# A fused first norm, a new order before w_o, and a last norm without GpSimd, in a two-block transformer on one Trainium2 core

## The reference, cut to what matters

```python
# 1. the first norm, and the input of all projections
u = rmsnorm(x, norm_mix) * (1.0 + scale1) + shift1      # shift1, scale1: first two rows of silu(c) @ ada_w + ada_b
... = split_cols(u @ w_in)                              # u is 512 x 1024
# 2. gates and branches, and the projection behind them
y_b = dsa_attention(...) @ w_br_b                       # 256 -> 1024
merged = gates[0] * y_a + gates[1] * y_b + gates[2] * y_c   # gates = sigmoid(u @ w_in[:, gates] + gate_b)
x = x + gate1 * (merged @ w_o)
# 3. the last norm
h = layer_norm(ALPHA * h + sq_relu_mlp(h, w1, w2), ln_g, ln_b)   # the output, 512 x 1024
```

## Time and profile before

| | us |
|---|---|
| median of 3 runs | 2599.14 |
| the three runs | 2591.30, 2599.14, 4247.02 |
| the profiled execution | 2593.75 |
| its span, first to last instruction | 2592.0 |
| TensorE busy (98%) | 2534.8 |
| VectorE busy (58%) | 1492.3 |
| ScalarE busy (44%) | 1144.0 |
| GpSimd busy (18%) | 454.5 |

### The profile page before, as it was taken

The page is one execution under the profiler, slowest core; times in us unless marked ns, Lnnn a source line. Parts: engine busy times, 40 slices in busy tenths (PEclk is TensorE's granted clock), DMA queues, the critical chain, the costliest instruction groups (busy, mean ns, idle before and its releaser), DMA issues.

```text
span 2592.0 us, 34147 instructions
## 1 busy us (share of the span) xinstructions
PE 2534.8 (98%) x13495; PEld 2126.6 (82%) x13495; DVE 1492.3 (58%) x2850; ACT 1144.0 (44%) x2214; POOL 454.5 (18%) x526
## 2 busy tenths in 40 slices
PE   6999999999999999999999999999999999999998
PEld 5876777798888988887897988889788887988888
DVE  5376977565433499888774743334735744743333
ACT  3365544354332435554654543324543553643322
POOL 4133342200000146553000100000000100100001
PEclk8999999999999999999999999999999999999999
DMA  9432234434433333213431333333221442333332
GB/s 271 122 98 74 66 100 122 120 94 127 130 95 94 90 90 98 58 58 94 129 87 50 89 98 98 98 98 88 82 82 33 130 123 57 90 98 97 96 93 89
DMA packets 470432, 253.02 MB, mean 98 GB/s; under 512 B 16458, under 2 KB 464670, under 8 KB 470271
## 3 DMA queue, kind: packets, MB, share of 16 engines
q1 hardware_dynamic: 466975, 243.18, 32.9%
q0 software_dynamic: 3152, 7.59, 1.3%
q10 hardware_dynamic: 144, 0.07, 0.0%
HBM read 247.99 MB, written 2.80 MB: 97 GB/s over the span
## 4 chain that ended last, share of the span: by engine, by line
PE 86%; DVE 6%; issue 3%; ACT 3%; DMA 1%; POOL 1%; SPq 0%; DVEq 0%; POOLq 0%; ACTq 0%
PE ps L1030 21%; PE ps L1032 20%; PE ps L1038 20%; PE ps L951 3%; PE ps L949 3%; PE ps L947 3%; PE ps L1188 1%; PE ps L965 1%; PE ps L1531 1%; PE ps L1553 1%; PE ps L967 1%; PE ps L978 1%; PE ps L1203 1%; DMA w_f<-in_w_in 1%; DVE w_r L2587 1%
## 5 line engine op out<-in xcount | busy, mean ns | idle before, releaser
L1030 PE MATMUL ps<-XH,wh 128*128 128x512 f32 (+2 forms) x1896 | 758.5, 400 | 8.6 <-ACT wh L1748 5.1
L1032 PE MATMUL ps<-XL,wh 128*128 128x512 f32 x1776 | 697.0, 392 | 0.5 <-DVE XL L2904 0.5
L2587 DVE TENSOR_TENSOR w_r<-w_f,wh 128x512 fp32r<-128x512 f32 (+1 forms) x625 | 409.2, 697 | 467.7 <-ACT wh L1748 467.1
L1748 ACT ACTIVATE wh<-w_f 128x512 fp32r<-128x512 f32 x787 | 446.3, 616 | 358.7 <-PE ps L1038 195.9
L1038 PE MATMUL ps<-XH,w_r 128*128 128x512 f32 (+2 forms) x1896 | 494.6, 392 | 2.9 <-DVE w_r L2587 2.9
L1030 PEld LDWEIGHTS ps<-XH,wh 128*128 128x128 f32 (+2 forms) x1896 | 356.7, 188 | 102.6 <-issue 16.0
L1038 PEld LDWEIGHTS ps<-XH,w_r 128*128 128x128 f32 (+2 forms) x1896 | 355.6, 188 | 82.7 <-DVE w_r L2587 5.6
L1032 PEld LDWEIGHTS ps<-XL,wh 128*128 128x128 f32 x1776 | 334.1, 188 | 73.3 <-issue 1.9
L1032 PE MATMUL ps<-arena_r,wh 128*128 128x512 f32 (+1 forms) x936 | 326.1, 359 | 0.0
L3758 POOL TENSOR_TENSOR w_r<-w_f,wh 128x256 fp32r<-128x256 f32 (+1 forms) x314 | 236.5, 784 | 362.8 <-ACT wh L1748 362.7
L1030 PE MATMUL ps<-arena_r,wh 128*128 128x512 f32 (+1 forms) x726 | 253.1, 363 | 2.6 <-ACT wh L1748 2.6
(11 more groups left out here) (430 smaller groups left out, 3654.6 us busy)
## 6 DMA issues: line engine op xcount, KB each, us to landing
w_f<-in_mlp_w SPq DMA_DIRECT2D x126, 512.0 KB, 4.1
w_f<-in_w_ff SPq DMA_DIRECT2D x63, 512.0 KB, 4.1
w_f<-in_w_in SPq DMA_DIRECT2D x49, 512.0 KB, 3.8
w_f<-in_ada_w SPq DMA_DIRECT2D x35, 512.0 KB, 4.1
w_f<-in_even_w_in SPq DMA_DIRECT2D x35, 512.0 KB, 3.7
w_f<-in_odd_w_in SPq DMA_DIRECT2D x23, 512.0 KB, 3.8
w_f<-in_even_w_out SPq DMA_DIRECT2D x16, 512.0 KB, 4.1
w_f<-in_xa_w_v SPq DMA_DIRECT2D x16, 512.0 KB, 4.1
```

Of the source, the lines that this page charges most:

```text
L1030: e.matmul(b, hi[:, k, :], xh, start=u.first and k == 0, stop=False)
L1032: e.matmul(b, hi[:, k, :], xl, start=False, stop=False)
L1748: e.activation(high_flat(u)[:, s], flat(u, 0)[:, s], ACT.Copy).then_inc(act.sem, act.up("high", u.n, i))
L2587: e.tensor_tensor(low[:, s], raw_[:, s], high[:, s], ALU.subtract).then_inc(dve.sem, dve.up("low", u.n, i))
```

## The change

Opening: VectorE forms hT x gain x root in one instruction and GpSimd's pass is gone; the shift is added by ScalarE while it rounds and by VectorE while it subtracts. ScalarE rounds both first weight blocks ahead of the chunks; VectorE lowers the first before the modulation is finished. TensorE does its second `mod_rows` ahead of the strip products. The 18 late loads move from ahead of project unit 2 to ahead of unit 6, the packs' turning from behind part 2 to behind part 7. Before w_o: the order becomes out 8, gate 12, ada, out 9, out 10, gate 13, ada, out 11, ada, out 12, gate 14, out 13, gate 15, out 14, out 15, and the splitting of `merged` and of the first w_o blocks is interleaved by hand behind gate 15. End: all eight second passes are on VectorE, in a new order. Context lines are left out in most places.

```diff
@@ -81,7 +81,6 @@
-SHARED_OUT = ((1, 0), (1, 1), (3, 0))
@@ -301,10 +300,8 @@
-    plans["branch b"] = []
-    for j in range(4):
-        plans["branch b"] += [b_outs[j], b_gates[4 + j]] + ([next(rest)] if j < 3 else [])
-    plans["branch b"] += b_outs[4:]
+    o, g = b_outs, b_gates
+    plans["branch b"] = [o[0], g[4], next(rest), o[1], o[2], g[5], next(rest), o[3], next(rest), o[4], g[6], o[5], g[7], o[6], o[7]]
...
     def before_norm(stage, units):
@@ -628,8 +625,8 @@
-        merged_after = {("gate", 2 * KC - 1): (0, 1), ("branch", KC + 4): (2, 3), ("branch", KC + 5): (4,),
-                        ("branch", KC + 6): (5,), ("branch", KC + 7): (6, 7)}
+        last_gate, last_outs = plans["branch b"][-3], plans["branch b"][-2:]
+        first_outs = plans["w_o"][:2]
@@ -755,7 +752,6 @@
-        out_by = lambda t, half: pool if (t, half) in SHARED_OUT else dve
@@ -870,7 +866,7 @@
-                if u is plans["project"][2]:
+                if u is plans["project"][6]:
@@ -889,7 +885,7 @@
-                w.wait_ge(out_by(t, half), "out", t, half)
+                w.wait_ge(dve, "out", t, half)
@@ -1154,6 +1150,7 @@
+            mod_rows(rows_bank, 1)
@@ -1162,8 +1159,6 @@
-            mod_rows(rows_bank, 1)
@@ -1174,7 +1169,7 @@
-                if i == 2:
+                if i == 7:
@@ -1732,6 +1727,13 @@
             def copy(o, i, *mark, scale=1.0):
...
+            def round_piece(u, i):
+                w.wait_ge(d_raw[u.raw], "unit", u.n)
+                w.wait_ge(pe, "unit", u.high_before.n)
+                s = slice(i * HIGH_PIECE, (i + 1) * HIGH_PIECE)
+                e.activation(high_flat(u)[:, s], flat(u, 0)[:, s], ACT.Copy).then_inc(act.sem, act.up("high", u.n, i))
...
             def round_ahead(n):
@@ -1998,12 +2000,12 @@
-            round_ahead(plans["mod"][-4].n)
+            round_ahead(plans["mod"][-1].n)
...
-                e.activation(XH[:, k, :], normed[:, k, :], ACT.Copy).then_inc(act.sem, act.up("xh", "X0", k))
-                if k == 0:
-                    round_ahead(plans["mod"][-1].n)
+                w.wait_ge(dve, "mod", 15)
+                e.activation(XH[:, k, :], normed[:, k, :], ACT.Identity, bias=shift(0, k), scale=1.0).then_inc(
+                    act.sem, act.up("xh", "X0", k))
@@ -2115,10 +2117,21 @@
-            for u in plans["branch b"]:
-                run_steps([u])
-                for k in merged_after.get((u.name, u.m), ()):
-                    merged_high(k)
+            run_steps(plans["branch b"][:-3])
+            round_ahead(last_gate.n)
+            assert units[rounded[0]] is first_outs[0]
+            rounded[0] += 2
+            merged_high(0)
+            for u in first_outs:
+                round_piece(u, 0)
+            evacuate(last_gate)
+            merged_high(1)
+            merged_high(2)
+            round_piece(first_outs[0], 1)
+            merged_high(3)
+            round_piece(first_outs[1], 1)
+            for k in range(4, KC):
+                merged_high(k)
@@ -2545,12 +2558,6 @@
-            def token_scaled(t, half):
-                w.wait_ge(dve, "out centered", t, half)
-                w.wait_ge(act, "token rstd", t // 2)
-                e.activation(ot_part(t, half), ot_part(t, half), ACT.Copy, scale=token_rstd[:, t:t + 1]).then_inc(
-                    act.sem, act.up("out scaled", t, half))
@@ -2559,13 +2566,10 @@
-            token_scaled(1, 0)
...
-            token_scaled(1, 1)
...
-            token_scaled(3, 0)
...
         def vector_program(e):
@@ -2573,6 +2577,13 @@
+            def lower_piece(u, i):
+                w.wait_ge(act, "high", u.n, i)
+                s = slice(i * HIGH_PIECE, (i + 1) * HIGH_PIECE)
+                e.tensor_tensor(flat(u, 1)[:, s], flat(u, 0)[:, s], high_flat(u)[:, s].bitcast(F32), ALU.subtract).then_inc(
+                    dve.sem, dve.up("low", u.n, i))
...
             def lower_ahead(n):
@@ -2880,6 +2891,14 @@
+            def scaled(k):
+                w.wait_ge(act, "rstd", "mix")
+                w.wait_ge(pe, "q", "mix")
+                w.wait_ge(dve, "gain", 0)
+                e.scalar_tensor_tensor(out=normed[:, k, :], in0=hT[:, k, :], scalar=gain(0, k), in1=stat[:, 0, :],
+                                       op0=ALU.mult, op1=ALU.mult).then_inc(dve.sem, dve.up("scaled", 0, k))
+            lower_ahead(plans["mod"][-4].n)
@@ -2888,23 +2907,16 @@
-            def scaled(k):
-                w.wait_ge(pool, "normed", k)
-                w.wait_ge(dve, "gain", 0)
-                w.wait_ge(dve, "mod", 15)
-                e.tensor_scalar(normed[:, k, :], normed[:, k, :], gain(0, k), shift(0, k), ALU.mult, ALU.add).then_inc(
-                    dve.sem, dve.up("scaled", 0, k))
-            scaled(0)
+                    scaled(0)
+            lower_ahead(plans["mod"][-1].n)
...
-                e.tensor_tensor(XL[:, k, :], normed[:, k, :], XH[:, k, :].bitcast(F32), ALU.subtract).then_inc(
+                w.wait_ge(dve, "mod", 15)
+                e.scalar_tensor_tensor(out=XL[:, k, :], in0=normed[:, k, :], scalar=shift(0, k),
+                                       in1=XH[:, k, :].bitcast(F32), op0=ALU.add, op1=ALU.subtract).then_inc(
...
-                if k < 2:
-                    lower_ahead(plans["mod"][-1 if k else -4].n)
@@ -3105,18 +3117,22 @@
-            for u in plans["branch b"]:
-                late = u.name == "branch" and u.m >= KC + 6
-                if late:
-                    evacuate(u)
-                else:
-                    run_steps([u])
-                if u.m < KC + 7 or u.name == "gate":
-                    for k in merged_after.get((u.name, u.m), ()):
-                        merged_low(k)
-                if late:
-                    lower_ahead(u.n)
-            for k in (6, 7):
+            run_steps(plans["branch b"][:-3])
+            lower_ahead(last_gate.n)
+            assert units[lowered[0]] is first_outs[0]
+            lowered[0] += 2
+            merged_low(0)
+            lower_piece(first_outs[0], 0)
+            evacuate(last_outs[0])
+            lower_piece(first_outs[1], 0)
+            merged_low(1)
+            merged_low(2)
+            evacuate(last_outs[1])
+            merged_low(3)
+            lower_piece(first_outs[0], 1)
+            merged_low(4)
+            lower_piece(first_outs[1], 1)
+            for k in range(5, KC):
@@ -3723,21 +3739,24 @@
             lower_ahead(last_tail[2].n)
             add_square_half(last_tail[0], 1)
             token_variance(0)
+            out_centered(0, 0)
             out_centered(1, 0)
-            out_centered(0, 0)
             residual(last_tail[1], 1)
             add_square_half(last_tail[1], 1)
             out_scaled(0, 0)
+            out_scaled(1, 0)
+            out_centered(0, 1)
             out_centered(1, 1)
-            out_centered(0, 1)
             residual(last_tail[2], 1)
             out_scaled(0, 1)
+            token_variance(1)
             out_centered(2, 0)
-            token_variance(1)
             out_centered(3, 0)
+            out_scaled(1, 1)
             out_centered(2, 1)
+            out_scaled(2, 0)
             out_centered(3, 1)
-            out_scaled(2, 0)
+            out_scaled(3, 0)
             out_scaled(2, 1)
             out_scaled(3, 1)
@@ -3829,17 +3848,8 @@
-            def normalize(k):
-                w.wait_ge(act, "rstd", "mix")
-                w.wait_ge(pe, "q", "mix")
-                e.tensor_tensor(normed[:, k, :], hT[:, k, :], stat[:, 0, :], ALU.mult).then_inc(pool.sem, pool.up("normed", k))
-            for k in range(2):
-                normalize(k)
...
-            for k in range(2, KC):
-                normalize(k)
@@ -4023,11 +4033,6 @@
-            for t, half in SHARED_OUT:
-                w.wait_ge(act, "out scaled", t, half)
-                w.wait_ge(d_final, "final")
-                e.tensor_tensor(ot_part(t, half), ot_part(t, half), out_bias[:, half * 512:(half + 1) * 512], ALU.add).then_inc(
-                    pool.sem, pool.up("out", t, half))
...
```

## The result

The changed kernel takes 2577.07 us, median of 8 runs (2572.25 to 2583.45), against 2594.66 for the kernel before in the same comparison. The ratio is 0.9934, with a 95% interval of 0.9918 to 0.995: 17 us (13 to 21) faster. One run of before, at 4247.02 us, is left out of the ratio. The profiled execution took 2581.69 us, with a span of 2579.9: 12.1 less than before. Forecast were 2581 us and 12.7 less.

The account below looks back on a forecast made before the run. TensorE, busy 98% of the span, was taken as the bound, with idle and half-clock time to win. Opening -6.9, packs -0.4, before w_o -6.2 and end +0.8 gave -12.7 from 2593.75: 2581 us, range 2574 to 2591.

Parts of the forecast that it names:

- What bounds the kernel: Whole kernel: TensorE works 98% of the span, and a stall on it is carried to the end nearly whole.
- Opening: Last modulation sums through the first pair: gain 6.9 us, bounds 4.0 and 8.9.
- the clock: Opening: one short drop to half clock behind the idle times, 2 us lost, bounds nothing and 4.9.
- The sums slow beside GpSimd: Opening: GpSimd's pass costs VectorE's sums about 1 us each; rival that they are not freed, 2584 us, chance 0.1.
- Packs and late loads: Project stretch: the 0.4 us wait in the packs goes; moving the late loads is worth nothing by itself.
- SP's queue as the new wait: Rival, project blocks: block 6 lands late and the kernel gets slower; chance 0.15, of which 0.03 above 2594 us.
- Before w_o: Branch stretch up to w_o: 8.1 us lost to waits and half clock, gain 6.2 us, bounds 3 and 8.1.
- Gate 14's wait: Before w_o: gate 14's load starts when gate 13 ends, so TensorE stands 1.1 to 1.5 us, taken as 1.3.
- small waits of w_o's start: Start of w_o: XL 3 and XL 5 come just at need beside GpSimd's additions; 0.6 us, 0 to 1.5.
- End: Last norm: four centrings and five second passes behind the variance; loss 0.8 us, from 0.3 gain to 1.5 loss.
- The sum: All terms together: 12.7 us less than the profiled 2593.75 us, so 2581 us.

Follow-up runs that it names:

- GpSimd busy beside them: Changed kernel plus eight GpSimd multiply passes, as removed by the change, written into a tile nobody then reads; 2582.72 us in one run.
- loads and packs back: Changed kernel with the 18 late loads again ahead of project unit 2 and the packs turned behind part 2; 2587.97 us in one run.
- opening alone: Kernel before with only the opening's edits: fused pass, first blocks, mod_rows, late loads and packs; median 2583.91 us, ratio 0.9957.
- end alone: Kernel before with only the last norm's second passes all on VectorE, in the new order; median 2594.72 us, ratio 0.9995.
- order before w_o alone: Kernel before with only the new order of branch b and the splitting of merged; median 2585.16 us, ratio 0.9962.
- again: Changed kernel run once more without any edit; 2577.28 us, ratio 0.9937 to the kernel before.

## Why the prediction was right, and where it was off

**What bounds the kernel:** right. What TensorE won at an edited place was still there at the end. At the second variance the changed kernel is 12.2 us ahead: 0.7 behind when the last three sums begin, -6.5 in A, -0.6 in B, +3.1 from the first scores to gate 12's tanh (with the half clock of 188 to 195 us, shown below), -6.2 in C, -2.3 from there to the first variance, -0.4 between the variances. The change doesn't touch the stretches of +0.7, +3.1 and -2.3. Together they give 1.5 us back, so it is in part luck that the spans differ by just what was forecast.

**Opening, forecast -6.9 (4.0 to 8.9):** A lost 6.5 us in one profile, 8.7 in the other. Line 1167 was forecast 2.7 us behind the start of the sums and came at 2.53; the sums themselves began 0.7 later than forecast, at 31.01, of which 0.55 is the five sums ahead of them, two of them slow beside GpSimd's squares (7.44 us in all, 6.89 before). The term that was mis-sized is the clock: I took 2 us lost in every execution, and the runs show 2.3 between an execution that loses it and one that doesn't. It also came earlier than forecast: line 1167 itself, taken at full clock (3.84), ran at half (5.46), so the first product with XL came at 41.79 and not at 40.2. Only 3.1 of the 6.5 us are won up to that product (13.85 us behind the start of the sums before, 10.78 now); the other 3.4 lie behind it, where the granted clock over 44 to 49 us is 0.93 and was 0.50. The prediction also weighed an estimate of 1.07 us for the fused pass and 1.75 per chunk, from the Trainium skill ("VectorE: DVE Perf Modes", section "The perf-mode tier table"), whose rows are for 2048 elements. At the 512 of this case the trace disagrees: a fused pass takes 0.75 us, and two passes take 1.32 us per chunk, the forecast's 1.3.

**The sums slow beside GpSimd:** right, and the experiment with GpSimd busy beside them shows it directly. The Trainium skill ("SBUF — State Buffer", section "Who interferes with whom") has it that a VectorE instruction with two inputs in SBUF contends with a GpSimd instruction that reads there; 2285 ns against 1275 agrees with that.

**Packs and late loads, forecast -0.4:** the term that was most under-sized. It rests on one wait of 0.4 us in one execution; three executions of the old opening have 0.44, 1.38 and 2.65, and B at 59.05 on average, so the move wins about 2.2 us, not 0.4. "Beyond the 0.4 this is worth nothing by itself" also fails against the new timing: with loads and packs back, B is 6.7 us longer.

**SP's queue as the new wait:** did not happen. Outside the opening's crowd 18 loads take 8.1 us to issue, not 16.5, and TensorE never waited for block 5 or 6.

**Before w_o, forecast -6.2 (3 to 8.1):** -6.2 in the profile (47.27 to 41.08). Gate 14's wait was 0.91, forecast 1.3, with the granted clock at 1.00 behind it as forecast, here and in the six other profiles with this gap. The reason given for it, that a gap so much shorter than 2.95 us does not halve the clock, is refuted by the opening: there gaps of 1.19 to 1.99 us were followed by half clock in six of seven profiles. So the outcome was right and its reason is open. The small waits of w_o's start were 0.23, forecast 0.6. By these two the stretch should have won 0.8 more (8.1 - 0.91 - 0.23 = 6.96); no single row carries that. The opening alone and the end alone, with the old order here, have C at 48.22 and 48.17; against the mean of the three the change wins 6.8.

**End, forecast +0.8 (-0.3 to +1.5):** -0.3. The variance came 10.32 us behind the first one instead of 10.73, 0.4 earlier (forecast 0.3), the nine passes took 6.10 us (forecast 6.3), and VectorE's last pass ended 16.42 instead of 15.97 behind the first variance, +0.45. The failing step is the last one: "the last store ends its issue at about 2590.3". SP's issuing ended 16.75 behind the variance before and 16.78 after. The forecast took VectorE's last pass (it ended at 2588.71 before) as what the last store waited for. It was not: SP issues the stores in order, and three of them, the last among them, stood behind GpSimd's tile (3, 0), whose add ran from 2586.36 to 2588.16. They went out in a row at 2588.2, 2588.6 and 2589.0, and the last one landed 2.5 us after its issue. In the changed kernel each store goes out as its pass ends, the last at 2577.4, and lands after 2.0 us. So SP's wait for GpSimd's tile covered VectorE's 0.45 us, and the gain of 0.3 is that the last store landed sooner. That it did so because it goes out alone is not shown. The end alone measured 0.9995 [0.9981, 1.0009], which holds both numbers.

**The sum, -12.7:** -12.1 between the two profiled spans. The medians differ by 17.6. Of the 5.5 us more, 4.6 are that the profiled execution of the changed kernel (2581.69, clock 0.995) was one of its slower ones. Of 47 executions of before (span and mean clock recorded) the mean span is 2592.5 at a clock of 0.9929; of 12 of the changed kernel 2575.7 at 0.9965. A straight line through all executions of all kernels, with one slope, gives 2.1 us less span per 0.001 of clock; at a clock of 0.995 before stands at 2588.0, the changed kernel at 2578.9. By this line about 9 us are won at equal clock, and about 8 because fewer stretches run at half. That second part is not all chance: by the granted clock of each us, A and C lose about 6.8 and 3.4 us to half clock in the profile before, and 3.4 and nothing in that of the changed kernel. The opening alone (0.9950) and the order before w_o alone (0.9952) each raise the clock over before by 0.002, the end doesn't (0.9924).

By stretches: the three profiles with the old opening have A at 29.42 on average, the four with the new one and sums as in the change (changed, again, opening alone, late loads back) 22.84. That is -6.6, and with -2.2 for B, -6.8 for C and -0.3 for E the sum is -15.9, where the medians show -17.6 and the forecast had -12.7. Of the 3.2 us between -12.7 and -15.9, 1.8 are the packs, 1.1 the end and 0.6 w_o, and the opening takes 0.3 back. These means are of three or four executions each, and 1.7 us of the medians' difference stay without a stretch.

## What to carry to other kernels

When a VectorE instruction lasts 1 us too long only in part of its executions, look at which GpSimd pass runs beside those. Moving that pass into VectorE can pay even where VectorE stands on the path. When TensorE is to arrive earlier somewhere, list the loads that it then meets and when they are issued: here the whole gain of the opening hung on 18 small loads and the packs' turning, priced at 0.4 us. And a wait behind a load is to be read in several executions: the same one was 0.44 us in one and 2.65 in another. Where orders are written out by hand, moving a unit forward moves its rounding and lowering forward on two in-order engines; look at what then stands behind a load that hasn't landed.

## What the runs showed of the hardware that was not expected

The granted clock does not follow from the gaps alone. The same three gaps of TensorE (1.19, 1.2 to 1.4, 1.16 us) were followed by half clock in one execution and by full clock in the next; of the seven profiles with this opening and GpSimd silent, six have line 1167 at half. Also a place that the change does not touch differed: behind one wait of 1.40 us, which both kernels have (line 1112, before 1116), the changed kernel's window was halved:

```profile
188.00:195.00 7.00, 7.00 (x18) 5.12 (x18) 6.56 (x21) 5.34 (x10) 2.00 (x3) 0.51 0.29 76
```

and the one of before was not:

```profile
194.00:201.00 7.00, 7.00 (x29) 5.20 (x29) 6.47 (x22) 5.57 (x10) 1.77 (x3) 1.00 0.29 76
```

The changed kernel's second execution had 0.81 there, behind the same 1.40 us. Seven us at half clock are 3.5 us, gained or lost through no edit; the 8 executions of the changed kernel in its first comparison lie 11 us apart, and their spans fall as their clock rises (2581.6 at 0.994, 2570.5 at 0.999). What decides whether a gap halves the clock was not found.
